# Two out-projection units and the last attention values inside the RWKV recurrence of a two-block kernel

## The chip, the cores and the metric

The kernel runs on one core of a Trainium2 chip. The metric is the device time of one execution in microseconds (us). The core's engines run side by side and meet by semaphores: TensorE (PE, matrix products into PSUM banks), VectorE (DVE), ScalarE (ACT), GpSimd (POOL) and SyncE (SP, which starts most of the DMAs).

## The reference, cut to what matters

The program computes two blocks on 256 tokens of width 1024, in fp32. The first block has two layers, the second one. The stage of this case is the mixer of the first block's layers:

```python
proj = (h @ w_in[l])                                    # 2944 columns
y_rwkv = _rwkv7_mixer(shifted proj, ...)                # 6 heads of 64, channels 0 to 383 of the mix
y_attn = _attention_mixer(proj, q_norm, k_norm)         # 6 heads of 64, channels 384 to 767
y_conv = _conv_mixer(proj, ...)                         # depthwise conv of 31 taps, layer norm, silu: 768 to 1023
x = x + concatenate([y_rwkv, y_attn, y_conv]) @ w_out[l]
```

The RWKV part is a recurrence over tokens on a 64x64 state for each head; its output is then normalised over each head's 64 channels, scaled, given a bonus and gated. Attention is a softmax over a banded score with a bias. The conv part ends in a layer norm over 256 channels. A SwiGLU feed-forward stands before and behind the mixer in each layer.

## The kernel before, in words

**Precision.** The large products are made from fp32 numbers split into a high part (ScalarE's copy to fp32r, `act_high`, L470) and a low part (VectorE's subtraction, `dve_low`, L475). `product` (L490) issues three matmuls for one product: high times high, high times low, low times high. Weights come into six slots by DMA from SP's queue.

**The mixer, `pe_mix`, `act_mix`, `dve_mix`, `pool_mixer`.** After the input projection, the recurrence is worked in chunks of 64 tokens (four chunks, two tiles of 128 tokens). For each chunk and head a triangular 64x64 matrix is inverted by products. `GROUPS_OF_CHAIN` lists sixteen steps i = 0 to 15 of this chain (eight products for two batches each, matmuls at L1530). A result of a "copy" product is taken out by ScalarE (L1821), that of an "add" by VectorE (L2022), that of a "move" by VectorE (L2015).

**Attention inside the chain.** The six heads of attention are laid into this chain by hand. For head h: `scores` on TensorE (L1180), `logits` on VectorE (bias and row maximum, L1218 to L1224), `exps` on ScalarE (L1245), `normalise` on VectorE (L1230, L1232), `turn` on TensorE (three transposes, L1190) and `copy` on ScalarE (L1252). For a pair of heads, `values` on TensorE (L1202, bank 1) and `out_` on ScalarE (L1257) follow. `turn(h)` waits for `p_ready`, `values(pair)` for `pt_done` of both heads. Heads 4 and 5 are turned at steps 11 and 14, `values(2)` stands at step 15. `prior_values` (L1504) are products of the recurrence laid into steps 11 and 12.

**The recurrence.** After the chain, TensorE makes `mat` (L1557), then for each of four chunks ch: the sa products (L1571, L1601, L1614), the new state (L1620, L1623, L1631), which VectorE scales (L2056), and `values_of` and `y_of` (L1564; L1571 and L1575), which build the outputs in banks 0 and 1. ScalarE copies sa (L1845) and makes scaled taps of the conv (L1787), which GpSimd adds up; VectorE also makes taps (L2043, L2045).

**The out projection.** The mix has eight channel groups of 128. It is multiplied by `w_out` in four groups k of two channel groups j, each in four parts (t, h): token tile t, output half h. One such part is an `out_unit(k, j, t, h)`: three 128x512 matmuls at L490 into bank 2, 3, 6 or 7. `out_ready(k, n)` waits for n counts of `mix_low` (the low parts of the mix) and for the low part of the weights. Group 0 (attention) lies inside the recurrence and behind it, group 1 holds channel group 3 (attention, j = 1) and 2 (RWKV, j = 0), group 2 the other two of RWKV, group 3 the conv.

**The tail.** After the last `y_of`, TensorE makes `variance` (L1651) and `gn_spread` (L1658) for two halves k with units of group 0 between them; then the conv's mean (L1671, `cl_mean`), units of group 1, the sum of squares (L1678, `cl_var`), and the rest. VectorE normalises and gates (L2075 to L2086, `mixr_ready`), takes the conv's mean off (L2089, `conv_dve`), makes the low parts of the RWKV mix (L2093, `mix_low`), then the low part of group 2's weights. GpSimd squares the centred values (L2151, `cl_sq`). ScalarE makes the high parts (L1867), the square root for the conv's norm (L1870, `cl_root`), the weights' high part for group 3, and the silu (L1875). In the second layer ScalarE then issues seven small DMAs for the second block (L2223), before the high part of the next feed-forward's first weights.

All orders are written out by hand: each engine's queue is in program order, and semaphores tie them together.

Of the kernel before, what the change touches and what calls it, by code (L numbers as in the profile page):

```python
# [16 lines left out]
F32 = mybir.dt.float32  # L17
# [174 lines left out]
def build(nc, a, out):  # L192
    packed_cols = constants()[1]
    ctx = ExitStack()
    with ctx:
# [1188 lines left out]
        def pe_mix(pe, uses, n_norm, l):  # L1384
# [124 lines left out]
            for i, (step, b) in enumerate(GROUPS_OF_CHAIN):  # L1509
# [23 lines left out]
                if i in (1, 3, 6, 9, 11, 14):  # L1533
                    attention.turn((1, 3, 6, 9, 11, 14).index(i))
# [12 lines left out]
                if i in (5, 10, 15):  # L1547
                    attention.values((5, 10, 15).index(i))
# [46 lines left out]
            for ch in range(4):  # L1595
# [21 lines left out]
                if ch < 3:  # L1617
                    bank = psum[6 + ch % 2]
                    if ch > 0:
                        pe.matmul(bank[:, 0:384], ident, state[:, ch - 1].rearrange("p a b -> p (a b)"), start=True,  # L1620
                                  stop=False, skip_group_check=True)
                    for h in range(NH1):
                        pe.matmul(bank[half(h), head(h)], tok[2][rows_, t, head(h)], tok[3][rows_, t, head(h)],  # L1623
                                  start=(ch == 0 and h < 2), stop=False, skip_group_check=True)
                    if ch == 0:
                        pe.wait_ge(S["mat_done"], 2 + past["mat_done"])
                        out_ready(0, 1)
                        out_unit(0, 0, 0, 0)
                    pe.wait_ge(S["sa_done"], ch + 1 + past["sa_done"])
                    for h in range(NH1):  # L1630
                        mm = pe.matmul(bank[half(h), head(h)], tok[1][rows_, t, head(h)],  # L1631
                                       satok[rows_, t, head(h)], start=False, stop=True, skip_group_check=True)
                    mm.then_inc(S["st_mm"], 1)
# [5 lines left out]
                if ch == 2:  # L1639
                    y_of(0)  # L1640
                    y_of(1)
                    values_of(1)
                if ch == 3:
                    y_of(2).then_inc(S["y_mm"], 1)
            pe.wait_ge(S["sa_done"], 4 + past["sa_done"])
# [27 lines left out]
            out_ready(1, 2)  # L1673
            for t, h in HALVES:
                out_unit(1, 1, t, h)
# [4 lines left out]
            out_ready(1, 4)  # L1680
            for h in range(2):
                out_unit(1, 0, 0, h)
# [16 lines left out]
        def act_mix(act, uses):  # L1699
# [116 lines left out]
            for i, (step, b) in enumerate(GROUPS_OF_CHAIN):  # L1816
# [5 lines left out]
                if i in (1, 3, 6, 9, 11, 14):  # L1822
                    attention.copy((1, 3, 6, 9, 11, 14).index(i))
# [14 lines left out]
            attention.out_(2)  # L1838
# [3 lines left out]
            for ch in range(4):  # L1842
# [3 lines left out]
                if ch == 0:  # L1846
                    act.wait_ge(S["mixa_ready"], 3 + past["mixa_ready"])
                    act_mixed(act, 3, 6, 2)
# [32 lines left out]
        def dve_mix(dve, uses, link):  # L1881
# [200 lines left out]
            for k in range(2):  # L2082
                dve.wait_ge(S["gn_spread"], k + 1 + past["gn_spread"])
                view = parity(mix[:, 0:3, :])[:, k]
                link(dve.tensor_tensor(view, view, psum[4 + k][:, 0:384].rearrange("p (c t n) -> p t c n", c=3, t=NT), mult))
                dve.tensor_tensor(view, view, parity(bonus)[:, k], add).then_inc(S["mixr_ready"], 1)  # L2086
            dve.wait_ge(S["cl_mean"], 1 + past["cl_mean"])
# [3 lines left out]
            for k in range(2):  # L2091
                dve.wait_ge(S["mix_high"], k + 3 + past["mix_high"])
                dve.tensor_tensor(parity(hT[1][:, 0:3, :])[:, k], parity(mix[:, 0:3, :])[:, k],  # L2093
                                  parity(hT[0][:, 0:3, :])[:, k].bitcast(F32), sub).then_inc(S["mix_low"], 1)
# [802 lines left out]
```

## Time and profile before

| | |
|---|---|
| median of 3 runs | 1378.06 us (1377.97 to 1378.1) |
| profiled execution | 1380.12 us, its span 1378.3 us |
| TensorE busy | 1348.3 us (98% of the span) |
| VectorE busy | 980.0 us (71%) |
| ScalarE busy | 741.7 us (54%) |
| GpSimd busy | 156.2 us (11%) |
| DMA | 230.57 MB, mean 167 GB/s |
| mean granted TensorE clock | 0.993 |

Times in the trace are from the span's start. The stage of this case runs from about 284 to 360 us in the first layer and from about 820 to 896 us in the second. Matmuls are pipelined and their ends are modelled, so that a row's start is firmer than its end.
### The profile page before, as it was taken

How to read it: one execution, taken by the hardware profiler on the slowest of the kernel's cores; microseconds unless marked ns; L12 is line 12 of the kernel's file. 1: busy time of each engine (PE TensorE's matmuls, PEld its weight loads, DVE VectorE, ACT ScalarE, POOL GpSimd, SP SyncE). 2: the span in 40 equal slices, each digit the busy share in tenths (PEclk: the TensorE clock that was granted, in tenths of full speed). 3: DMA queues.
4: the chain of work that ended last, by engine and by line, in shares of the span. 5: the costliest groups of instructions: out<-in, count | busy, mean ns of one | idle time of the engine just before them, and what ended most of it. 6: DMA issues, size and time to landing. Idle time of an engine off the chain costs nothing.

```text
span 1378.3 us, 24757 instructions
## 1 busy us (share of the span) xinstructions
PE 1348.3 (98%) x9701; PEld 1168.5 (85%) x9701; DVE 980.0 (71%) x1310; ACT 741.7 (54%) x1048; POOL 156.2 (11%) x156
## 2 busy tenths in 40 slices
PE   9999999989999999999999998999999999999997
PEld 7888889977888888888888987788888997788885
DVE  6666666777776666766656766876666665998787
ACT  6444457465744445644447656564444445755553
POOL 3000000097000000000000048300000033000000
PEclk9999999999999999999999999999999999999999
DMA  9756355123475645755529121465553953456630
GB/s 339 265 184 197 112 178 174 34 92 114 150 251 189 197 130 184 261 189 183 183 67 298 55 93 34 127 225 197 187 187 106 305 183 106 152 187 216 197 133 31
DMA packets 170483, 230.57 MB, mean 167 GB/s; under 512 B 4687, under 2 KB 151815, under 8 KB 170149
## 3 DMA queue, kind: packets, MB, share of 16 engines
q1 hardware_dynamic: 167920, 223.75, 49.6%
q10 hardware_dynamic: 1877, 5.59, 1.1%
q8 instruction: 56, 0.92, 0.3%
q0 software_dynamic: 608, 0.12, 0.1%
q14 instruction: 22, 0.18, 0.0%
HBM read 228.39 MB, written 2.63 MB: 168 GB/s over the span
## 4 chain that ended last, share of the span: by engine, by line
PE 89%; DVE 5%; ACT 3%; issue 1%; POOL 1%; ACTq 0%; POOLq 0%; DVEq 0%
PE banks L490 37%; PE banks L658 27%; PE banks L662 14%; PE banks L1530 2%; DVE down_lo L475 1%; DVE gate_lo L475 1%; PE banks L613 1%; PE banks L941 1%; PE banks L1180 1%; PE banks L1393 1%; PE banks L1333 1%; PE banks L1190 1%; DVE up_lo L475 1%; PE banks L1464 0%; PE banks L1202 0%
## 5 line engine op out<-in xcount | busy, mean ns | idle before, releaser
L658 PE MATMUL banks<-hT,up_hi 128*128 128x512 f32 x880 | 220.8, 393 | 0.0
L475 DVE TENSOR_TENSOR down_lo<-w_down,down_hi 128x2048 fp32r<-128x2048 f32 (+1 forms) x65 | 147.8, 2273 | 93.2 <-ACT down_hi L470 93.2
L737 ACT ACTIVATE work<-banks 128x256 f32<-128x256 f32 x176 | 66.8, 384 | 258.6 <-PE banks L662 258.2
L658 PE MATMUL banks<-hT,gate_hi 128*128 128x512 f32 x800 | 199.8, 392 | 0.0
L470 ACT ACTIVATE down_hi<-w_down 128x2048 fp32r<-128x2048 f32 (+1 forms) x65 | 123.6, 1902 | 115.9 <-PE banks L490 115.9
L658 PEld LDWEIGHTS banks<-hT,up_hi 128*128 128x128 f32 x880 | 158.2, 189 | 29.2 <-issue 0.6
L475 DVE TENSOR_TENSOR up_lo<-w_up,up_hi 128x2048 fp32r<-128x2048 f32 x72 | 164.5, 2285 | 15.9 <-ACT up_hi L470 15.9
L475 DVE TENSOR_TENSOR gate_lo<-w_gate,gate_hi 128x2048 fp32r<-128x2048 f32 x64 | 146.9, 2296 | 36.7 <-ACT gate_hi L470 36.6
L658 PEld LDWEIGHTS banks<-hT,gate_hi 128*128 128x128 f32 x800 | 147.0, 188 | 28.4
L490 PE MATMUL banks<-down_hi,ff_hi 128*128 128x512 f32 x400 | 156.2, 391 | 0.0
L490 PE MATMUL banks<-down_lo,ff_hi 128*128 128x512 f32 x400 | 156.2, 391 | 0.0
L490 PE MATMUL banks<-down_hi,ff_lo 128*128 128x512 f32 x400 | 155.6, 389 | 0.0
L743 DVE TENSOR_TENSOR work<-banks,work 128x256 f32<-128x256 f32 x176 | 73.1, 421 | 108.4 <-ACT work L737 108.4
L470 ACT ACTIVATE up_hi<-w_up 128x2048 fp32r<-128x2048 f32 x72 | 136.6, 1897 | 6.2 <-PE banks L490 6.2
L470 ACT ACTIVATE gate_hi<-w_gate 128x2048 fp32r<-128x2048 f32 x64 | 122.5, 1914 | 12.1 <-PE banks L490 9.3
L662 PEld LDWEIGHTS banks<-hT,up_lo 128*128 128x128 f32 x880 | 119.8, 190 | 10.3 <-DVE up_lo L475 1.9
L662 PE MATMUL banks<-hT,up_lo 128*128 128x256 f32 x880 | 123.0, 283 | 0.6 <-DVE up_lo L475 0.6
L662 PEld LDWEIGHTS banks<-hT,gate_lo 128*128 128x128 f32 x800 | 109.1, 190 | 7.8
L662 PE MATMUL banks<-hT,gate_lo 128*128 128x256 f32 x800 | 111.5, 282 | 0.0
L490 PEld LDWEIGHTS banks<-down_hi,ff_lo 128*128 128x128 f32 x400 | 75.1, 188 | 16.0
L490 PEld LDWEIGHTS banks<-down_hi,ff_hi 128*128 128x128 f32 x400 | 75.3, 188 | 14.3
L490 PEld LDWEIGHTS banks<-down_lo,ff_hi 128*128 128x128 f32 x400 | 75.3, 188 | 13.7
(388 smaller groups left out, 2217.4 us busy)
## 6 DMA issues: line engine op xcount, KB each, us to landing
w_up<-in_ffn_w_up_dram SPq DMA_DIRECT2D x44, 1024.0 KB, 5.4
w_down<-in_ffn_w_down_dram SPq DMA_DIRECT2D x44, 1024.0 KB, 5.2
w_gate<-in_ffn_w_gate_dram SPq DMA_DIRECT2D x43, 1024.0 KB, 5.4
w_up<-in_w_in_dram SPq DMA_DIRECT2D x12, 1024.0 KB, 9.5
w_gate<-in_w_up_dram SPq DMA_DIRECT2D x11, 1024.0 KB, 5.0
w_up<-in_w_up_dram SPq DMA_DIRECT2D x11, 1024.0 KB, 5.1
w_down<-in_w_down_dram SPq DMA_DIRECT2D x11, 1024.0 KB, 5.0
w_down<-in_w_in_dram SPq DMA_DIRECT2D x9, 1024.0 KB, 8.4
```

Source lines behind the costliest of these rows:

```text
L470: act.activation(staged[kind][0][:, 0:cols], slot[sl][:, 0:cols], ACT.Copy).then_inc(high[sl], 1)
L475: dve.tensor_tensor(staged[kind][1][:, 0:cols], slot[sl][:, 0:cols], staged[kind][0][:, 0:cols].bitcast(F32), ALU.subtract).then_inc(split ...
L490: mm = pe.matmul(out_, lhs(l_), rhs(r_), start=first and i == 0, stop=last and i == 2, **kw)
L613: pe.matmul(psum[j][:, :], w[0][:, c, j * P:(j + 1) * P], hpair[:, :, c, :], start=c == 0, stop=False)
L658: pe.matmul(bank[:, :], w[0][:, c, at], hpair[:, :, c, :], start=c == 0, stop=False)
L662: mm = pe.matmul(bank[:, 0:SEQ], w[1][:, c, at], hT[0][:, c, :], start=False, stop=c == KC - 1)
L737: act.activation(to[:, q, j * SEQ:(j + 1) * SEQ], psum[2 * q + j][:, SEQ:], ACT.Copy)\
L743: dve.tensor_tensor(to[:, q, at], psum[2 * q + j][:, 0:SEQ], from_[:, q, at], ALU.add)\
L941: mm = pe.transpose(place(places, c)[:, t * P:(t + 1) * P], x[:, t, c * P:(c + 1) * P], ident)
L1180: mm = pe.matmul(bank[:, q_at.start:q_at.start + k_at.stop], q[:, q_at], k[:, k_at], start=True, stop=True)
L1190: mm = pe.transpose(psum[self.b_turn[h % n]][:, i * P:(i + 1) * P], self.logit[:, h % 2, i * P:(i + 1) * P], ident)
L1530: mm = pe.matmul(view(out_[to, j // 3, head(j % 3)]), chain[lhs][at, q, :], view(right), start=True, stop=True)
```

## The change

In each of the first block's two layers:

- Heads 4 and 5 of attention are turned, and their transposes copied by ScalarE, at chain steps 12 and 15 and no longer at 11 and 14.
- `values(2)` leaves step 15 of the chain. It stands in the recurrence's first chunk, before the wait for `mat_done`. ScalarE's `out_(2)` moves from before the mat copies to behind the first sa copy.
- `out_unit(1, 1, 0, 0)` is put at the end of chunk 2 of the recurrence, with the wait for group 1's weights, and `out_unit(1, 1, 0, 1)` at the end of chunk 3, between `y_of(2)` and `y_of(3)`. They leave the tail.
- In the tail, `out_unit(1, 0, 0, 0)` and `out_unit(1, 0, 0, 1)`, with their wait for all four low parts, come before `cl_var` and no longer behind it.
- On VectorE the two low parts of the RWKV mix come before the centring of the conv, and no longer behind it.

```diff
@@ -1530,8 +1530,8 @@
                         mm = pe.matmul(view(out_[to, j // 3, head(j % 3)]), chain[lhs][at, q, :], view(right),
                                        start=True, stop=True)
                     mm.then_inc(S["copy_mm" if kind == "copy" else "add_mm"], 1)
-                if i in (1, 3, 6, 9, 11, 14):
-                    attention.turn((1, 3, 6, 9, 11, 14).index(i))
+                if i in (1, 3, 6, 9, 12, 15):
+                    attention.turn((1, 3, 6, 9, 12, 15).index(i))
                 if i == 7:
                     pe.wait_ge(S["mixa_ready"], 1 + past["mixa_ready"])
                     turn(6)
@@ -1544,8 +1544,8 @@
                     prior_values(i - 11)
                 if i in (1, 7):
                     attention.scores(1 if i == 1 else 2)
-                if i in (5, 10, 15):
-                    attention.values((5, 10, 15).index(i))
+                if i in (5, 10):
+                    attention.values((5, 10).index(i))
             inv = chain["INV"]
 
             pe.wait_ge(S["copy_done"], COPIES + past["copy_done"])
@@ -1623,6 +1623,7 @@
                         pe.matmul(bank[half(h), head(h)], tok[2][rows_, t, head(h)], tok[3][rows_, t, head(h)],
                                   start=(ch == 0 and h < 2), stop=False, skip_group_check=True)
                     if ch == 0:
+                        attention.values(2)
                         pe.wait_ge(S["mat_done"], 2 + past["mat_done"])
                         out_ready(0, 1)
                         out_unit(0, 0, 0, 0)
@@ -1640,8 +1641,11 @@
                     y_of(0)
                     y_of(1)
                     values_of(1)
+                    out_ready(1, 2)
+                    out_unit(1, 1, 0, 0)
                 if ch == 3:
                     y_of(2).then_inc(S["y_mm"], 1)
+                    out_unit(1, 1, 0, 1)
             pe.wait_ge(S["sa_done"], 4 + past["sa_done"])
             y_of(3).then_inc(S["y_mm"], 1)
 
@@ -1670,16 +1674,15 @@
             for c in range(2):
                 mm = pe.matmul(psum[0][:, 0:SEQ], ones, mix[:, 6 + c, :], start=(c == 0), stop=(c == 1))
             mm.then_inc(S["cl_mean"], 1)
-            out_ready(1, 2)
-            for t, h in HALVES:
-                out_unit(1, 1, t, h)
+            for h in range(2):
+                out_unit(1, 1, 1, h)
+            out_ready(1, 4)
+            for h in range(2):
+                out_unit(1, 0, 0, h)
             pe.wait_ge(S["cl_sq"], 1 + past["cl_sq"])
             for c in range(2):
                 mm = pe.matmul(psum[1][:, 0:SEQ], ones, proj[:, CG + c, 1:], start=(c == 0), stop=(c == 1))
             mm.then_inc(S["cl_var"], 1)
-            out_ready(1, 4)
-            for h in range(2):
-                out_unit(1, 0, 0, h)
             out_ready(2, 4)
             for j in range(2):
                 for t, h in HALVES:
@@ -1819,8 +1822,8 @@
                         view = nonzero(step, rhs)
                         act.wait_ge(S["copy_mm"], n + 1 + past["copy_mm"])
                         act.activation(view(of_batch(dst, b)), view(in_banks(m)), ACT.Copy).then_inc(S["copy_done"], 1)
-                if i in (1, 3, 6, 9, 11, 14):
-                    attention.copy((1, 3, 6, 9, 11, 14).index(i))
+                if i in (1, 3, 6, 9, 12, 15):
+                    attention.copy((1, 3, 6, 9, 12, 15).index(i))
                 if i in (8, 9):
                     turned(i - 2)
                 if i in (12, 13):
@@ -1835,7 +1838,6 @@
                     act.wait_ge(S["mixa_ready"], 2 + past["mixa_ready"])
                     act_mixed(act, 4, 5)
             act.wait_ge(S["add_mm"], ADDS + past["add_mm"])
-            attention.out_(2)
             for i, k in enumerate((1, 0)):
                 act.wait_ge(S["mat_mm"], i + 1 + past["mat_mm"])
                 act.activation(mat_[:, k, :], psum[2 + k][:, 0:384], ACT.Copy).then_inc(S["mat_done"], 1)
@@ -1844,6 +1846,7 @@
                 act.wait_ge(S["sa_mm"], ch + 1 + past["sa_mm"])
                 act.activation(satok[rows_, t, :], psum[4 + t][rows_, 0:384], ACT.Copy).then_inc(S["sa_done"], 1)
                 if ch == 0:
+                    attention.out_(2)
                     act.wait_ge(S["mixa_ready"], 3 + past["mixa_ready"])
                     act_mixed(act, 3, 6, 2)
                 if ch in (0, 2):
@@ -2084,14 +2087,14 @@
                 view = parity(mix[:, 0:3, :])[:, k]
                 link(dve.tensor_tensor(view, view, psum[4 + k][:, 0:384].rearrange("p (c t n) -> p t c n", c=3, t=NT), mult))
                 dve.tensor_tensor(view, view, parity(bonus)[:, k], add).then_inc(S["mixr_ready"], 1)
+            for k in range(2):
+                dve.wait_ge(S["mix_high"], k + 3 + past["mix_high"])
+                dve.tensor_tensor(parity(hT[1][:, 0:3, :])[:, k], parity(mix[:, 0:3, :])[:, k],
+                                  parity(hT[0][:, 0:3, :])[:, k].bitcast(F32), sub).then_inc(S["mix_low"], 1)
             dve.wait_ge(S["cl_mean"], 1 + past["cl_mean"])
             for c in range(2):
                 ins = dve.scalar_tensor_tensor(mix[:, 6 + c, :], psum[0][:, 0:SEQ], -1.0 / 256, mix[:, 6 + c, :], mult, add)
             ins.then_inc(S["conv_dve"], 1)
-            for k in range(2):
-                dve.wait_ge(S["mix_high"], k + 3 + past["mix_high"])
-                dve.tensor_tensor(parity(hT[1][:, 0:3, :])[:, k], parity(mix[:, 0:3, :])[:, k],
-                                  parity(hT[0][:, 0:3, :])[:, k].bitcast(F32), sub).then_inc(S["mix_low"], 1)
             dve_low(dve, uses, OUT_SLOTS[2], kind=OUT_KINDS[2])
             dve.wait_ge(S["cl_root"], 1 + past["cl_root"])
             link(dve.reciprocal(proj[:, CG + 1, 1:], proj[:, CG, 1:]))
```

## Rows read from the trace of the kernel before

**Rows 1.** The page's chain of work that ended last: shares of the span by engine.
```profile
PE 89%; DVE 5%; ACT 3%; issue 1%; POOL 1%; ACTq 0%; POOLq 0%; DVEq 0%
```

**Rows 2.** Windows, first layer: length, busy us (instructions) per engine, PEclk, DMA share, GB/s.
```profile
312.00:316.00 4.00, 2.94 (x100) 2.27 (x92) 3.39 (x9) 1.48 (x4) 3.84 (x3) 1.00 0.53 154
...
332.00:334.00 2.00, 2.00 (x34) 1.80 (x31) 2.00 (x2) 0.90 (x2) 1.84 (x3) 1.00 0.54 181
...
336.00:338.00 2.00, 2.00 (x9) 1.81 (x9) 1.94 (x5) 0.52 (x2) 1.44 (x2) 0.50 0.00 0
```

**Rows 3.** Windows, second layer, same columns.
```profile
872.00:874.00 2.00, 2.00 (x9) 1.85 (x8) 1.93 (x5) 0.63 (x2) 1.34 (x2) 0.50 0.00 0
```

**Rows 4.** Timeline of TensorE, chain's end, first layer: start, us, instruction, idle before.
```profile
308.52 0.55 PE L1190 MATMUL banks<-cst,work 128*128 128x128 f32 x3 [0.83 <-DVE work L1232]
...
315.14 0.88 PE L1202 MATMUL banks<-spare,work 128*64 128x128 f32 x12
315.94 1.38 PE L1557 MATMUL banks<-work,w_gate 64*64 64x64 f32 x45
```

**Rows 5.** Timeline of VectorE, chain's end, first layer.
```profile
309.94 2.70 DVE L475 TENSOR_TENSOR down_lo<-w_gate,down_hi 128x2048 fp32r<-128x2048 f32 x1
...
315.11 0.36 DVE L2022 TENSOR_TENSOR work<-banks,work 128x192 f32<-128x192 f32 x1
```

**Rows 6.** Chain of waits, first layer: start, us, what, matmul count.
```profile
324.26 1.59 PE banks L490 x6
...
330.19 0.89 PE banks L490 x3
...
334.50 0.62 PE banks L1651 x6
335.12 1.24 PE banks L490 x3
336.36 1.08 PE banks L1651 x6
337.44 1.48 PE banks L490 x3
...
339.56 1.28 PE banks L490 x3
...
341.48 1.23 PE banks L1671 x4
342.71 2.75 PE banks L490 x12
345.45 0.87 PE banks L1678 x4
```

**Rows 7.** Timeline of VectorE, recurrence and tail, first layer.
```profile
325.47 2.77 DVE L475 TENSOR_TENSOR up_lo<-w_up,up_hi 128x2048 fp32r<-128x2048 f32 x1 [0.67 <-ACT up_hi L470]
...
342.74 0.76 DVE L2089 SCALAR_TENSOR_TENSOR mix<-banks,mix 128x256 f32<-128x256 f32 x2
343.42 1.86 DVE L2093 TENSOR_TENSOR hT<-mix,hT 128x384 fp32r<-128x384 f32 x2
345.20 2.28 DVE L475 TENSOR_TENSOR gate_lo<-w_down,gate_hi 128x2048 fp32r<-128x2048 f32 x1
...
352.06 0.68 DVE L1156 TENSOR_TENSOR hT<-mix,hT 128x512 fp32r<-128x512 f32 x1
```

**Rows 8.** Timeline of GpSimd, tail, first layer.
```profile
343.58 1.28 POOL L2151 TENSOR_TENSOR proj<-mix 128x512 f32<-128x512 f32 x1 [5.72 <-DVE mix L2089]
```

**Rows 9.** Timeline of ScalarE, tail, second layer.
```profile
882.25 0.48 ACT L1870 ACTIVATE proj<-banks,small 128x256 f32<-128x256 f32 x1 [3.13 <-PE banks L1678]
...
884.55 1.28 ACT L1875 ACT_TABLE_LOAD   x1
...
889.71 1.92 ACT L470 ACTIVATE gate_hi<-w_gate 128x2048 fp32r<-128x2048 f32 x1 [2.09 <-PE banks L490]
```

**Rows 10.** Timeline of TensorE, tail, second layer.
```profile
895.21 1.09 PE L941 MATMUL banks<-cst,x 128*128 128x128 f32 x8 [0.53 <-DVE x L856]
```

## The prediction

> **What bounds the kernel now.** I read the page first. Its chain of work gives TensorE 89% of the span [rows 1], so a time saved elsewhere counts only where TensorE waits. The edit lies in one stage that runs once in each of the first block's two layers: the chain products that invert the 64x64 matrices, the recurrence behind them, and the out projection. The second copy follows the first by some 536 us with nearly the same times, so I work on the first copy and carry the result over, except at the end of the stage, where the two differ.
>
> The windows come next. In the chain TensorE is idle for about a quarter of a stretch (2.94 us busy of 4.00), in the recurrence it is full (2.00 of 2.00) [rows 2]. So a piece that is put into the recurrence finds no hole. The same view shows the one odd thing here: the granted clock is 1.00 up to 334 us, 0.50 in 336 to 338; by 342.7 it is back, as twelve unit matmuls at 0.23 us each show [rows 2, 6]. The second layer has the same fall [rows 3]. These are TensorE's two levels, 2.4 and 1.2 GHz. Before the fall it ran only narrow products: two y_of groups (outputs 64 columns wide) and the 6-column variance. It did not idle. Last I read the chain of waits through the tail, piece by piece, because nearly every duration of the sum is there [rows 6].
>
> **Part 1, heads 4 and 5 turned one step later, values(2) moved into the recurrence.** Before, values(2) (0.88 us, spacing to the next group 0.80) stands between the last chain product and the first mat product, which starts at 315.94. The last thing mat needs is the VectorE add at 315.11, 0.36 long, so 315.47 [rows 4, 5]. That add follows other VectorE work whose order is unchanged, so it doesn't move. The fifth head's turn now costs a wait of 0.83 us on VectorE ahead of 308.52 [rows 4]. Moving it frees nothing: TensorE then comes sooner to a product that needs a bank which VectorE's add leaves only at 309.9, when its 2.70 us low part begins, and the next one waits for VectorE behind that [rows 5]. After the change the fifth head's turn lies behind the chain product of step 12 and the sixth's behind the last one, in front of this add's end: mat can start at 315.47 plus about 0.14 (the gap of 0.14 to 0.15 between an engine's end and the next matmul is usual here), 315.61: **0.33 us gained**. values(2) is then done within the recurrence, where TensorE is full: **0.80 us paid**. Queued behind its wait (probT of both heads copied) are only mat_done's wait and the first out unit. ScalarE's copy of its result goes behind the first sa copy; it delays ScalarE's scaled taps and through them its second sa copy a little, and I cost that at nothing because TensorE has the ident product and the state products of the next chunk in hand. Should that cover be gone, it costs some 0.3 us a layer.
>
> **Part 2, two out units in the recurrence.** A unit is three fp32r 128x512 matmuls. Two in a row cost 1.59 us, one among small products 0.89 [rows 6]. The first new one stands beside an old one: 1.59 - 0.89 = 0.70. The second stands alone between y_of(2) and y_of(3): 0.89. Together **1.59 us paid**, with no wait that it fills. Their weights' low part is ready at 325.47 + 2.77 = 328.2 [rows 7], and TensorE comes there after 330, so the new wait on the slot costs nothing.
>
> **Part 3, the clock.** With a 512-column unit between the y groups, the run of narrow work that came ahead of the fall is cut in two. I take it that the clock stays at 2.4 GHz. At half clock now: three units of 1.24, 1.48 and 1.28, and a variance of 1.08 [rows 6]. At full clock they take 3 x 0.89 and 0.62: 5.08 - 3.29 = **1.79 us saved**; the two groups of three transposes and the mean product save a few tenths more, of which about 0.3 ahead of the mean product.
>
> The Trainium skill speaks against this. Its page "TensorE: Matmul & The Clock Gate", section "What's actually happening", says that the gate follows how busy the engine has been of late, and the section "Why this matters for your kernels" names idle gaps as what to avoid. By that, work that leaves TensorE as busy as before would change nothing. The rows disagree: no idle time ahead of the fall, while the stretch 312 to 316, a quarter idle, kept 1.00. What this would make of the time is the first rival.
>
> **Sum to the second gn_spread** (its end is the start of the mean product, 341.48 [rows 6]): -0.33 + 0.80 + 1.59 - 1.79 - 0.3 = **about 0**. So the whole clock gain is spent on the 2.4 us that moved in ahead of it.
>
> **Part 4, what lies behind.** Before, four units (2.75 us) follow the mean product, then cl_var, 0.87, ending 346.32, then two units; group 2 starts at 347.7. In parallel VectorE does the centring, 0.76 from 342.74, the two low parts, 1.86, and gate_lo, 2.28 from 345.20, ending 347.48 [rows 6, 7]. So TensorE and VectorE arrive there within 0.2 us of each other. After the change TensorE has two units fewer, 1.4 us, but VectorE has the same work. That gain becomes waits: mix_low 4 comes at 342.7 + 1.86 = 344.6, the centring ends at 345.3, GpSimd's square (1.28 [rows 8]) at 346.65, cl_var from 346.7 to 347.55. gate_lo ends at 347.5 as before. Group 2 thus starts at about 347.6: **-0.1 us in the first layer**.
>
> But cl_var is now 347.55 - 346.32 = 1.2 us later, since the centring was moved behind the low parts. ScalarE's square root, its 1.91 us slot copy and the table load before the silu all queue behind it. In the first layer this has room: the last low part of the mix ends at 352.74 [rows 7], and TensorE wants it after twelve units of 0.69 from 346.3, at 354.6. In the second layer it has none: the square root starts at 882.25, the table load at 884.55, then come silu, the mix copy and seven DMA issues on ScalarE's queue, and the gate_hi copy starts only then, at 889.71. Through it the low part and the residuals are late, and TensorE already waits at 895.21, for 0.53 us [rows 9, 10]. All of that moves by 1.2: **+1.2 us in the second layer**. The DMA issues themselves only move with the queue.
>
> The profiled execution spans 1378.3 us (1380.12 with what lies around it), and the median of the runs is 1378.06; differences are carried over one for one. -0.1 + 1.2 = +1.1: **1379.2 us**.
>
> **Rivals.**
> (a) The clock falls all the same, at the same place or in the stretch behind it. For: y_of(3) and the variance are still narrow, and still together some 1.9 us. Against: the unit between them and y_of(2). The sum to gn_spread is then -0.33 + 0.80 + 1.59 = +2.1 a layer: +2.0 in the first, +3.3 in the second, **1383.4 us, slower**. If only one layer falls, about 1381.3. It decides from the point where one fall returns, since 1.1 + 2.1 is over 2.76 us.
> (b) The trace's matmul ends are modelled, so the recurrence may hold small waits that the busy share hides, and the three moved pieces may fill them. If all 2.4 us were hidden, gn_spread would be bound by VectorE's gn_rows instead, about 1.9 us earlier than now: -1.9 and -1.9 + 1.2, **1375.4 us, faster**. For: TensorE passes between engines at every chunk. Against: the pieces start one behind the other with the pitch of their weight loads.
> (c) The edit does not do what it says at the end: cl_var's delay is swallowed by ScalarE's slack, and the two layers give -0.1 each: **1377.9 us**, no change. Against: silu starts right at the end of the table load 884.55 + 1.28 = 885.83 [rows 9].
>
> **Numbers.** 0.2% is 2.76 us, about what a measurement of this kernel can tell from no change. Chances: the forecast 0.56 (of it 0.02 beyond that bound, with the clock kept but a further 1.7 us of waits), (a) 0.24, (b) 0.12, (c) 0.08. Faster 0.12, same 0.54 + 0.08 = 0.62, slower 0.26. The likeliest case alone spans 1377.6 to 1380.6: each single unit's 0.2 us switching price may be nothing (-0.5 a layer), and ScalarE's cover may be gone. The range must take in (a) and half of (b): 1376.0 to 1383.6.
>
> **What would show it.** Right: granted clock 1.00 from 316 to 348 and in the second layer; mat products from about 315.6; gn_spread's end within 0.3 us of 341.5; a TensorE wait of near 0.8 us for the low part and one of 0.7 for the square's product; the stage's gate_hi copy in the second layer 1.2 us later than 889.71. Wrong: a clock of 0.50 anywhere in the stage, (a); gn_spread's end under 340.5, (b); gate_hi in the second layer not late, (c). The prediction would fall most by the clock: nothing in this trace varies the work ahead of the fall, so that it goes away is an inference from one pattern seen twice.

## The result: slower by half a per cent, 7.3 us

The changed kernel takes **1385.37 us** (median of 6 runs, 1384.07 to 1391.09) against 1378.08 us (6 runs, 1377.9 to 1382.77) for the kernel before on the same chip: ratio 1.0050, 95% interval [1.0028, 1.0071]. That is slower, and above the range that was given. A second set of 8 runs gave 1385.4 us, ratio 1.0055 [1.0035, 1.0074]. The profiled execution took 1385.28 us, with a span of 1383.4 us. One execution of a part kernel further down (the two units, square on ScalarE) took 2207 us at a mean granted clock of 0.555, and is left out of that kernel's median and ratio.

I start with the shares of the chain of work, as in [rows 1]:

```profile
PE 88%; DVE 5%; ACT 3%; POOL 1%; issue 1%; DMA 0%; ACTq 0%; POOLq 0%; SPq 0%; DVEq 0%
```

Nothing new there: at this grain 7 us in 1383 don't show. So the stage has to be read. The windows of the changed kernel at the two places where the clock had fallen before answer to [rows 2, 3] (length, then busy us and instruction counts of TensorE, its weight loads, VectorE, ScalarE and GpSimd, the granted clock, DMA share, GB/s):

```profile
336.00:338.00 2.00, 2.00 (x23) 1.52 (x22) 2.00 (x2) 0.49 (x1) 1.84 (x3) 1.00 0.00 0
...
874.00:876.00 2.00, 2.00 (x25) 1.56 (x23) 1.97 (x3) 0.43 (x2) 1.84 (x3) 1.00 0.00 0
```

The clock did stay at 1.00 among the y products, as forecast. The loss is behind them. The chain of waits through the tail of the second layer, the same view as [rows 6] (start, us, what, count), names it:

```profile
883.25 3.03 POOL proj L2154
```

GpSimd's square of the centred convolution stands on the chain with 3.03 us. I had costed it at 1.28 [rows 8]. TensorE's timeline at that place, in both layers (start, us, instruction, in brackets the idle time before it and what ended it):

```profile
348.65 1.67 PE L1684 MATMUL banks<-proj,cst 128*128 128x256 f32 x4 [2.10 <-POOL proj L2154]
...
882.56 0.50 PE L490 MATMUL banks<-up_hi,hT 128*128 128x512 f32 x1 [0.38 <-DVE hT L2092]
...
886.32 1.13 PE L1684 MATMUL banks<-proj,cst 128*128 128x256 f32 x4 [2.10 <-POOL proj L2154]
...
900.27 1.09 PE L941 MATMUL banks<-cst,x 128*128 128x128 f32 x8 [1.88 <-DVE x L856]
```

TensorE waits 0.38 us for the low part (I had said 0.8), **2.10 us** for the square (0.7), and then 1.88 us at the end of the stage, where [rows 10] had 0.53. VectorE and GpSimd beside each other in the changed kernel, second layer:

```profile
882.42 0.75 DVE L2096 SCALAR_TENSOR_TENSOR mix<-banks,mix 128x256 f32<-128x256 f32 x2
883.09 2.28 DVE L475 TENSOR_TENSOR gate_lo<-w_down,gate_hi 128x2048 fp32r<-128x2048 f32 x1
```

```profile
883.25 3.02 POOL L2154 TENSOR_TENSOR proj<-mix 128x512 f32<-128x512 f32 x1 [5.19 <-DVE mix L2096]
```

The square now starts 0.16 us behind VectorE's 2.28 us subtract gate_lo and lasts 3.02 us. In the kernel before it started beside the two 128x384 low parts, and took 1.28 us while these took 1.86 together [rows 7, 8]. The move of the centring behind the low parts changed its neighbour.

**The accounts.** For a comparison free of the clock I profiled both kernels once more. The kernel before then spanned 1376.0 us and showed none of its two falls; the same windows as in [rows 2, 3]:

```profile
336.00:338.00 2.00, 2.00 (x13) 1.64 (x12) 1.97 (x4) 0.79 (x3) 1.55 (x2) 1.00 0.00 0
...
872.00:874.00 2.00, 1.13 (x7) 0.65 (x7) 1.93 (x6) 1.74 (x1) 1.03 (x1) 1.00 0.00 0
```

So the fall on which the sum rested comes in some executions of the kernel and not in others. It is no accident of one execution either: a kernel further down with the same order on TensorE up to the tail (the kernel before with the square on ScalarE) has its falls at the same two places, from 334 and from 870 us. Its window in the first layer:

```profile
336.00:338.00 2.00, 2.00 (x9) 1.81 (x9) 1.93 (x5) 0.56 (x2) 1.27 (x1) 0.50 0.00 0
```

The second row of before's second profile holds something else: TensorE is busy only 1.13 of 2.00 us. Its timeline in this profile says why:

```profile
873.31 0.55 PE L1658 MATMUL banks<-cst,spare 128*128 128x128 f32 x3 [0.87 <-DVE spare L2080]
```

At full clock the kernel before waits 0.87 us for VectorE's group-norm rows. At half clock TensorE came later, and the wait was not there to be seen.

The table gives the stage in pieces, second layer: when TensorE starts mat, the first variance, the conv's mean product, cl_var, and the first turn behind the out projection (the transposes at L941), in us from the first chain product. Only the first profile in it has half clock inside these pieces.

```
                        mat     variance  mean product  cl_var   turn behind the stage
before, 1st profile     29.43   47.81     54.75         58.76    72.79   (half clock from 48.8)
before, 2nd profile     29.37   47.75     52.97         56.67    71.10
after, 1st profile      28.99   49.62     53.76         60.31    74.26
after, 2nd profile      29.00   49.65     53.79         60.32    74.26
```

And the two spans, 1376.0 (before, second profile) and 1383.4 (after, second profile), differ by 7.40 us: ahead of the stage -0.44, first layer's stage +1.82, between the two +1.47, second layer's stage **+3.16**, behind it +1.39. The stretches of the +1.47 and +1.39 hold no changed instruction. Each is a fall of the clock, at 753 and at 900 us, with TensorE full while it lasts. The second, in a window of the changed kernel's second profile (same columns; clock 0.57):

```profile
900.00:904.00 4.00, 4.00 (x13) 3.15 (x12) 2.35 (x5) 2.58 (x8) 0.00 (x0) 0.57 0.61 215
```

### The profile page after: what moved, and what is told of

The parts are those of the page before. It is cut to its first block, busy times and chain, and to the rows that moved or that the text cites. A ratio compares the mean times of both kernels' runs of the same rounds, so it can differ in the third digit from the quotient of the medians.

```text
span 1383.4 us, 24757 instructions
## 1 busy us (share of the span) xinstructions
PE 1346.1 (97%) x9701; PEld 1165.4 (84%) x9701; DVE 979.7 (71%) x1310; ACT 741.9 (54%) x1048; POOL 160.3 (12%) x156
## 4 chain that ended last, share of the span: by engine, by line
PE 88%; DVE 5%; ACT 3%; POOL 1%; issue 1%; DMA 0%; ACTq 0%; POOLq 0%; SPq 0%; DVEq 0%
PE banks L490 36%; PE banks L658 27%; PE banks L662 14%; PE banks L1530 2%; PE banks L613 1%; PE banks L1180 1%; PE banks L1393 1%; PE banks L1333 1%; DVE down_lo L475 1%; PE banks L1190 1%; DVE up_lo L475 0%; DVE gate_lo L475 0%; PE banks L941 0%; DMA w_gate<-in_ffn_w_gate_dram 0%; PE banks L1464 0%
```

## The experiments

Times are medians. Ratios are to runs of the kernel before on the same chip (1377.7, 1377.58 and 1377.74 us in the groups); they are an estimate over all the runs and not the quotient of the two medians, from which they differ by up to 0.001. "Stage" is the length in the second layer as in the table's last column, which is 71.10 before and 74.26 after.

### Does the tail's new order carry the loss?

The changed kernel with the old order of the tail: low parts of the mix behind the centring again, units (4) behind cl_var.

```diff
@@ VectorE
-            for k in range(2):
-                dve.wait_ge(S["mix_high"], k + 3 + past["mix_high"])
-...
             dve.wait_ge(S["cl_mean"], 1 + past["cl_mean"])
...
+            for k in range(2):
+                dve.wait_ge(S["mix_high"], k + 3 + past["mix_high"])
+...
@@ TensorE
-            out_ready(1, 4)
-            for h in range(2):
-                out_unit(1, 0, 0, h)
             pe.wait_ge(S["cl_sq"], 1 + past["cl_sq"])
...
+            out_ready(1, 4)
+            for h in range(2):
+                out_unit(1, 0, 0, h)
```

> Changed kernel with its tail put back to the old order: the conv's centring before the low parts on VectorE, cl_var before the units (1,0,0,h) on TensorE. Attention move and the two units in the recurrence stay. Theory A (the tail's order is the cause: the GpSimd square runs beside the weights' low part and takes 3.03 us where it took 1.28, and cl_var with all behind it waits): the square takes 1.3 us again and the time is within 1.5 us of the kernel before, 1376.5 to 1379. Theory B (the work moved into the recurrence is the cause): still 1382 or more. Theory C (only the place where TensorE's clock falls differs): the time follows the count of half-clock stretches, not the order.

Measured: 1379.23 us (12 runs), ratio 1.0009 [0.9995, 1.0024]; stage 71.84, that is 2.42 shorter than the changed kernel's. The square takes 1.28 us again, and TensorE's wait for it is:

```profile
879.73 1.13 PE L1681 MATMUL banks<-proj,cst 128*128 128x256 f32 x4 [1.28 <-POOL proj L2154]
```

Some 6 of the 7.7 us are gone with the order of the tail. The converse, the tail's order put into the kernel before and nothing else (the same diff read backwards):

> Kernel before with the tail's new order alone (low parts ahead of the centring on VectorE, units (1,0,0,h) ahead of cl_var on TensorE); attention and the four units of (1,1) as before. Theory A: the GpSimd square again takes about 3.0 us and cl_var starts 6.5 us after the mean product, where the kernel before has 4.0; the stage is 1.5 to 2.5 us longer in each layer, 1381 to 1383. Theory B (the moved work is the cause): the same as the kernel before within 1 us.

Measured: 1381.54 us (12 runs), ratio 1.0025 [1.0012, 1.0038], slower by 3.8 us; stage 73.47, 2.37 longer than before's. GpSimd and TensorE in it:

```profile
877.75 3.02 POOL L2151 TENSOR_TENSOR proj<-mix 128x512 f32<-128x512 f32 x1 [5.18 <-DVE mix L2093]
```

```profile
880.83 1.13 PE L1681 MATMUL banks<-proj,cst 128*128 128x256 f32 x4 [1.45 <-POOL proj L2151]
```

Added to the kernel before or taken from the kernel after, the order costs the same 2.4 us in the second layer's stage. So the tail's cost doesn't depend on the other parts there. In the medians the two differ, 3.8 and 6.2 us; what is left over lies outside that stage, and is taken up under the sum below.

### Is it the square, and the neighbour on VectorE?

Two ways to take the square out of gate_lo's company. First, ScalarE squares instead of GpSimd:

```diff
-            pool.wait_ge(S["conv_dve"], 2 + past["conv_dve"])
-            pool.tensor_tensor(proj[:, CG:CG + 2, 1:], acc, acc, mult).then_inc(S["cl_sq"], 1)
...
+            act.wait_ge(S["conv_dve"], 2 + past["conv_dve"])
+            act.activation(proj[:, CG:CG + 2, 1:], mix[:, 6:8, :], ACT.Square).then_inc(S["cl_sq"], 1)
             act.wait_ge(S["cl_var"], 1 + past["cl_var"])
```

> Changed kernel, whole, but the conv's square (two channel groups, 128x512) is made by ScalarE and no longer by GpSimd. Theory A: the square takes some 0.6 us, cl_var comes about 2.3 us sooner after the centring; TensorE is then held by group 2's weights instead, so the first layer gains 1 to 2 us and the second 2 us: 1381 to 1382.5 against 1385.3 for the changed kernel. Theory B or C: no gain, 1384 to 1386.

Measured: 1379.8 us (12 runs), ratio 1.0011 [0.9998, 1.0025]; stage 71.78, 2.48 shorter than the changed kernel's. The gain is larger than expected (1381 to 1382.5 us). ScalarE's row:

```profile
877.81 0.64 ACT L1873 ACTIVATE proj<-mix 128x512 f32<-128x512 f32 x1 [1.29 <-DVE mix L2098]
```

Second, GpSimd keeps the square, and VectorE waits for it before gate_lo:

```diff
+            dve.wait_ge(S["cl_sq"], 1 + past["cl_sq"])
             dve_low(dve, uses, OUT_SLOTS[2], kind=OUT_KINDS[2])
```

> Changed kernel; VectorE waits for the conv's square before it starts the low part of group 2's weights, so that GpSimd and VectorE don't run at once there. Nothing else differs. Theory A (the square is slow because it runs beside that VectorE instruction): the square takes 1.28 us again, cl_var starts 1.7 us sooner after the mean product (4.8 in place of 6.5 us), the low part 1.4 us later; the second layer's stage is 1.5 us shorter (72.7 against 74.3 us), the median 1382 to 1384 against 1385.4. If the square stays at 3.0 us (it is slow by itself at that place): the stage grows by 1.5 us, 1387 to 1389.

Measured: 1381.01 us (12 runs), ratio 1.0023 [1.0012, 1.0034]; stage 72.28, 1.98 shorter. The median is under the 1382 to 1384 expected, and the square fell below the 1.28 us of the old order. The square and gate_lo in it:

```profile
878.40 1.04 POOL L2155 TENSOR_TENSOR proj<-mix 128x512 f32<-128x512 f32 x1 [5.18 <-DVE mix L2096]
```

```profile
879.47 2.29 DVE L475 TENSOR_TENSOR gate_lo<-w_down,gate_hi 128x2048 fp32r<-128x2048 f32 x1 [1.15 <-POOL proj L2155]
```

This is the run that settles the mechanism. The instruction, its engine, its shape and everything ahead of it are as in the changed kernel. Only its neighbour is gone, and it takes 1.04 us instead of 3.02. Neither is a chance value: the square took 3.02 in both layers of all four profiles in which gate_lo is its neighbour and nothing holds VectorE back, and 1.28 or 1.29 in both layers of the five profiles in which GpSimd squares in the old order. The price, 1.15 us on VectorE, comes back as a wait of 1.28 us of TensorE for gate_lo, which is why it wins less than ScalarE's square.

### What do the two other parts cost?

The attention part alone in the kernel before (heads 4 and 5 a step later, values(2) in the recurrence):

```diff
-                if i in (1, 3, 6, 9, 11, 14):
-                    attention.turn((1, 3, 6, 9, 11, 14).index(i))
+                if i in (1, 3, 6, 9, 12, 15):
+                    attention.turn((1, 3, 6, 9, 12, 15).index(i))
...
                     if ch == 0:
+                        attention.values(2)
                         pe.wait_ge(S["mat_done"], 2 + past["mat_done"])
```

> Kernel before with the attention part alone: heads 4 and 5 turned at steps 12 and 15, the last values in the recurrence. By the changed kernel's second layer, mat starts 0.6 us sooner and the values cost 0.8 later: theory A +0.2 a layer, 1378.5, with the clock falling as in the kernel before. Theory B: +1 us a layer or more, 1380 to 1381. Theory C: anything between 1378 and 1383 by where the clock falls.

Measured: 1376.7 us (12 runs), ratio 0.9987 [0.9977, 0.9997]; stage 70.88. The part is a small gain, where the expectation had a small loss, 1378.5 us. The two units alone, tail in the old order:

```diff
                     values_of(1)
+                    out_ready(1, 2)
+                    out_unit(1, 1, 0, 0)
                 if ch == 3:
                     y_of(2).then_inc(S["y_mm"], 1)
+                    out_unit(1, 1, 0, 1)
...
-            out_ready(1, 2)
-            for t, h in HALVES:
-                out_unit(1, 1, t, h)
+            for h in range(2):
+                out_unit(1, 1, 1, h)
```

> Kernel before with two units of group 1 moved into the recurrence alone, tail in the old order. Theory A: the clock stays full past the y products, 1.6 us of units moved in against about 2.1 us of clock won back ahead of the mean product: 1376.5 to 1378. Theory B: +1 us a layer or more. If the clock falls at the old place despite the unit between the y groups: about 1381.

Measured: 1377.78 us (12 runs), ratio 1.0006 [0.9991, 1.0022]; stage 71.09. The medians don't differ, but four of the twelve runs took 1382.5 to 1384.1 us, at a mean granted clock of 0.992 or 0.993; of the 35 runs of the kernel before beside them two did. The profile is of one of the short runs, so where these four lost their clock isn't known. Together (that is the first experiment) they give a stage of 71.84, 0.74 over before's, where the two alone give -0.22 and -0.01. The pieces show why they don't add up. From the variance to the mean product the kernel before takes 5.22 us, with the wait of 0.87 in it; with the attention part 4.52, with the units 4.14, with both 4.13. The wait is spent once. Either part hides in it; the two together, 1.85 us later at the variance, find only 1.09 to hide in, and 0.76 is left.

### Combinations without the collision

The kernel before with the square on ScalarE, and with the units or both parts besides (old tail in all):

> Kernel before with the conv's square on ScalarE alone. In its order the square has no collision and TensorE never waits for it, so theory A expects the kernel before within 0.5 us: 1377.2 to 1378.2. A gain of 1 us or more would say that the 1.4 us that the attention part with this square gained come from the square.

Measured: 1377.21 us (11 runs), ratio 0.9996 [0.9987, 1.0005]; stage 72.67, with the fall in it. The profiled execution is one of the long ones, 1379.64 us.

> The two units alone, old tail, square on ScalarE. The units alone came out level with the kernel before (1377.8 against 1377.7): they fill TensorE's wait of 0.87 us ahead of the group norm's spread and cost 1.4 us ahead of it. Square hidden: 1377 to 1378, no more than 0.7 us from the kernel before.

Measured: 1377.09 us (11 runs), ratio 0.9998 [0.9982, 1.0013]; stage 70.46. Three of the eleven took 1381.9 to 1383.8 us at a clock of 0.991 or 0.992, and none of the 35 runs beside them more than 1380.3: the units again, with a longer time in some runs.

> Attention part and the two units, old tail, square on ScalarE. At full clock the attention part and the units together made the second layer's stage 0.7 us longer than before, since the units alone already fill TensorE's wait of 0.87 us for the group norm's rows and the values then find no hole. The square is hidden in this order: 1378.5 to 1379.5, as with the square on GpSimd.

Measured: 1379.07 us (11 runs), ratio 1.0007 [0.9998, 1.0016]; stage 71.04. None of the three can be told from the kernel before. In the old order the square's neighbour is not what hurts. The last combination is the attention part and the square on ScalarE, without the units:

> Kernel before with the attention part alone, and the conv's square on ScalarE. The tail order is the old one, where the square took 1.28 us on GpSimd without a collision and was done before TensorE asked for it. Theory A: ScalarE's square hides as well as GpSimd's did, so no more than the attention part alone gives: 1376 to 1377. If ScalarE delays the high part of the mix or of the weights: 1377 to 1378.

Measured: **1376.13 us** (12 runs), ratio 0.9980 [0.9969, 0.9992]. It beats both kernels, by 1.6 us and by 9.3 us. Its interval overlaps that of the attention part alone, and the square alone gave nothing, so the gain is put down to the attention part. Beside the attention part the units cost more than they bring: with them the same kernel took 1379.07 us, and the two intervals don't meet.

### Does the new wait bring the clock down?

The second profiles, of the changed kernel and of the kernel before, were there for the clock; both are shown above.

> The changed kernel itself, timed on the same chip as the part kernels. Theory A: in the second layer from the first chain product to the first turn behind the out projection 74.3 us at full clock, as in its first profile, 2.4 more than with the old tail; the median 2.5 to 6 us over the kernel before, 1380 to 1384, the spread from where the clock falls. If it comes out within 1 us of the kernel before, the first measurement was an accident of the clock.

> The kernel before itself, for a second profile. If the place where the clock falls is a matter of the execution and not of the program, this profile shows the falls elsewhere than at the end of the y products or not at all, and the stage then takes about 70.5 us in each layer in place of 72.4 and 72.8. If it is a matter of the program, it shows the same two falls.

Measured: 1385.4 us (8 runs), above the 1380 to 1384 expected, with the stage of 74.26 as expected; 1377.8 us (one run), with no fall in either layer and stages of 72.05 and 71.10 us where about 70.5 was expected. Outside the program's last microseconds the kernel before had half clock in two places in its first profile and in none in its second; the changed kernel in three places in either. In the first profile these are at 216.0, 311.6 and 349.1 us, in the second at 347.1, 753.2 and 900.0. That at 311.6 lies in the chain of the first layer, where the change moved a turn, and the changed kernel with the old tail has one at 310.7; it made mat start at 30.14 us into the stage, where the second profile has 28.73. One of the three comes back, in the first layer close behind the long wait: at 349.1 us in one profile and 347.1 in the other, with cl_var starting at 348.65 and 345.81. The windows ahead of it, first profile, show the hole and then the fall (clock 0.76 in the second row):

```profile
344.00:348.00 4.00, 2.20 (x9) 1.16 (x7) 3.58 (x5) 0.25 (x1) 2.42 (x1) 1.00 1.09 355
348.00:352.00 4.00, 3.35 (x9) 2.68 (x10) 1.13 (x1) 1.64 (x2) 0.60 (x1) 0.64 0.76 255
```

To test it I filled the hole in the changed kernel with two products of constants whose results are discarded:

```diff
+            for _ in range(2):
+                pe.matmul(psum[1][:, :], ident, cst[:, 0:512], start=True, stop=True)
             pe.wait_ge(S["cl_sq"], 1 + past["cl_sq"])
```

> Changed kernel; two 128x512 products into a bank that holds nothing then are put ahead of TensorE's wait for the conv's square, so that this wait of 2.1 us is no idle time. They are discarded and computed from constants. Theory A1 (the wait also makes the clock fall more often; the stage's own length is 3.2 us a layer and the clock gives the rest of the difference of 7.7 us): stage in the second layer 74.3 us as in the changed kernel, mean granted clock back to 0.996, median 1383 to 1384. Theory A2 (the falls come elsewhere, the wait has no part in them): median 1385 to 1386 with the clock at 0.993 as in the changed kernel.

Measured: 1383.74 us (6 runs, 1380.14 to 1385.52), ratio 1.0043 [1.0031, 1.0055]. The hole shrinks from 2.10 to 0.38 us, with cl_var no sooner (60.31 us into the first layer's stage; in the second, 59.30, where the whole chain ran 1.0 us shorter ahead of mat, which no edit accounts for):

```profile
878.70 1.88 PE L1683 MATMUL banks<-cst 128*128 128x512 f32 x4
...
880.96 1.13 PE L1686 MATMUL banks<-proj,cst 128*128 128x256 f32 x4 [0.38 <-POOL proj L2156]
```

The fall behind it is absent from this profile (it has one, at 895.9 us). The mean granted clock of its runs was 0.993 to 0.998, where the changed kernel's 14 runs had 0.987 to 0.995. From cl_var to the turn the first layer now takes 12.19 us, in the changed kernel's second profile 13.82: the fall there cost 1.63. Both point to the wait, and the gain of 1.7 us is about what one fall costs. But the two intervals overlap, and in the second layer the same wait of 2.1 us has no fall behind it in either profile of the changed kernel. So this is suggested, not shown.

The second wait that the change lengthened has the same look. At the stage's end in the second layer, TensorE waits 1.88 us (before: 0.58 in its second profile). Falls stood at 900.1 us in the changed kernel's second profile, 895.9 with the hole filled, and 896.0 with the tail's order alone; these three turns behind the stage started at 898.85, 894.90 and 894.77, so each fall came 1.0 to 1.3 us behind a wait of 1.9. None of the eleven profiles whose wait there is 1.22 us or less has a fall at this place. The changed kernel's first profile has the wait of 1.88 and not the fall, so the wait makes it likelier and doesn't force it. No edit tested this wait.

## Why the prediction was wrong, point by point

Two terms of the sum failed. The clock gain of 2.1 us a layer was booked against a median in which it was mostly there already, and GpSimd's square was priced at 1.28 us where it took 3.02, so that cl_var held TensorE back in both layers, where the forecast had -0.1 us in the first and +1.2 in the second. The moved pieces themselves were priced nearly right. The points in order:

- **Part 1, the attention part: right on the chain.** mat starts 0.38 us sooner (forecast 0.33; second layer), and values(2) costs 0.81 (0.80). The sign named for the first layer, mat at about 315.6 us (29.1 behind the first chain product), stands at 28.73 in the second profile and, behind the fall in the chain, at 30.14 in the first. The part as a whole is a gain of 1.0 us in the median, because of a cover that the sum didn't know (the point on the mean product).
- **Part 2, two units paid 0.70 + 0.89: nearly right as prices, 0.69 and 0.75 measured.** The second layer shows all of parts 1 and 2 ahead of the variance: the variance starts 1.87 us later, and -0.38 + 0.81 + 0.69 + 0.75 is 1.87.
- **Part 3, the clock: the first step that failed, wrong in what it compared with.** The clock stayed at 1.00 among the y products in both layers of both profiles of the changed kernel, as forecast. But I booked 2.1 us a layer as a gain against a median whose executions mostly don't pay them: before's own second profile has no fall there, and its stage is 71.10 against 72.79 us, so a fall cost 1.7. The sign that I passed over was on the table: the profiled execution of before, 1380.12 us, was 2 us above its median, and I called differences one for one. Whether the added units keep the fall away is open. It is absent from all nine profiles that have a unit between the y products, but also from four of the six that have none; two of six against none of nine is too little to tell.
- **"About 0" at the mean product** failed with that. Against the profile that the sum was worked from, the mean product came 0.99 us sooner (53.76 against 54.75), since more was won from half to full clock than booked. Against a kernel before at full clock it is +0.79 in the second layer: 1.87 later at the variance, less 1.08 of VectorE's group-norm rows, whose wait the half clock had hidden in [rows 6]. Rival (b) supposed hidden waits to be filled; there was one, but of a size of 1.1 us, and it was used up.
- **Part 4, the mis-sized term: GpSimd's square, 1.28 us booked and 3.02 measured.** My forecast had cl_var 5.2 us behind the mean product (346.7 less 341.48). The changed kernel needs 6.55, that is 1.3 more. The square grew by 3.02 - 1.28 = 1.74, and the centring ended 0.4 sooner than booked, 3.40 behind the mean product and not 3.8; 1.74 - 0.4 is the 1.3. The 0.4 has the same root with the other sign: the 1.86 us booked for VectorE's two low parts were a price beside the square, and away from it they took 1.23, with a short wait between them. Against the kernel before the stretch grew by 2.85 (from 3.70, second profile) or 2.54 (from 4.01, the first). The step that failed was taking the duration from [rows 8] while moving the instruction beside another neighbour. The trace had a row that says so, on GpSimd's timeline in the kernel before, first layer, beside the 2.77 us up_lo subtract of [rows 7]:

```profile
326.17 2.88 POOL L2139 TENSOR_TENSOR proj<-proj,par 128x460 f32<-128x460 f32 x1
```

  This GpSimd operation, of about the square's size, takes 2.88 us beside such a subtract; the median of its line's thirty is 1.00.
- **"-0.1 us in the first layer": wrong.** I had cl_var ending with gate_lo, so that nothing was lost there. With the square at 3.02, cl_var is what holds group 2 in both layers. The first layer's stage went from 72.05 to 73.87 us. An estimate of its own part is +1.4: the +1.82, less the 1.63 of the fall in it, plus 1.23 that TensorE idled once in mat in before's second profile, with no releaser named.
- **Second layer, ScalarE's chain: right mechanism, wrong size.** It queues behind cl_var as said, and all of it moved. The rows that answer to [rows 9]:

```profile
887.50 0.48 ACT L1873 ACTIVATE proj<-banks,small 128x256 f32<-128x256 f32 x1 [5.58 <-PE banks L1684]
...
894.77 1.92 ACT L470 ACTIVATE gate_hi<-w_gate 128x2048 fp32r<-128x2048 f32 x1 [1.92 <-issue]
```

  Counted from the first chain product, the gate_hi copy is 1.5 us later than in the profile that I had (68.76 against 67.29), where I had forecast 1.2; but that profile has the fall in it. cl_var is 3.64 us later than in before's second profile, and the end of the stage 3.16, with TensorE waiting 1.88 us there.
- **Rival (a)**, at 1383.4 us, came nearest, and was right in part. It had the fall "at the same place or in the stretch behind it". At the same place it didn't come. Behind it, it did in the first layer, in both profiles (349.1 and 347.1 us), so the sign that I had named against the forecast, a clock of 0.50 anywhere in the stage, was there; it cost 1.63 us, where (a) had 2.1. In the second layer's stage there was none. The square, the larger part of the loss in the stage, stands in no rival.
- **The sum as it is now.** The stage gives +3.16 in the second layer and about +1.4 in the first, 4.6 us of a median difference of 7.3 to 7.7. In parts: the tail alone +3.8, both other parts together +1.5, 5.3 in sum. The remaining 2 to 3 us are of the size of the falls outside the stage, which cost 1.47 and 1.39 in the second profile. The mean granted clock of the changed kernel's runs is lower (0.987 to 0.995; before's 24 runs beside them have a median of 0.996), so it has more half clock. What sets it off is open: the two long waits are suggested by the last experiment, and the units by the long runs of the two kernels that have the units and no wait of over 1.1 us at these two places.

## What to carry to other kernels

The duration of a GpSimd instruction is that of its company: when it is moved, take its price from a row in which the new neighbour runs beside it, and look through the trace for such a row. Take the price of the VectorE instruction that it leaves from such a row too. A fall of the clock in one profile is not a term of a sum before a second profile, or the distance from the profiled execution to the median, has shown that the other executions have it too. And a wait that hides one inserted piece doesn't hide two: cost them against one cover, together.

## What the runs showed of the hardware

**GpSimd beside VectorE.** One and the same GpSimd instruction, a 128x512 fp32 product from SBUF to SBUF, took 1.04 us alone, 1.28 beside two 128x384 VectorE subtracts, and 3.02 beside one 128x2048 subtract of 2.28 us that had started 0.16 us earlier. 2.28 - 0.16 + 1.04 = 3.16, so within 0.14 us it behaves as if it had stood still until VectorE was done and had then run alone. The 1.28 comes out the same way, as an estimate: it started 0.16 us behind the first low part of 0.55 us, and 0.55 - 0.16 + 1.04 = 1.43, within 0.15. Where the square is first, VectorE pays. The two low parts in the kernel before (shortest, median and longest in ns):

```profile
L2093 DVE TENSOR_TENSOR hT<-mix,hT x4: 547/972/1397, 343.4 to 879.8; 128x384 fp32r<-128x384 f32 x4
```

The second took 1.40 us with the square under way; with the square on ScalarE each took 0.55. gate_lo kept its 2.28 in the collision that it had begun first. The Trainium skill, page "SBUF — State Buffer", section "Who interferes with whom", says that a VectorE instruction with two SBUF inputs contends with a GpSimd instruction that reads SBUF, and that this contention is an exclusive lock. The traces agree, by the 3.16 against 3.02 above and by the second low part.

**The clock.** It fell from 1.00 to 0.50 in before's first profile while TensorE had been busy for 2.00 of every 2.00 us [rows 2], and not in the second, with the same instructions; a kernel with the same order up to there had it at the same two places again. Falls in the changed kernel's profiles stood behind its waits of 2.1 and 1.9 us, but also at 311 us, in the chain, and at 216 and 753 us, where nothing was changed; two of the part kernels have one at 749 and 751 us too. One cost 1.4 to 1.5 us where TensorE was full, and 1.6 to 1.7 in the stage.
